# Output gate tiles computed inside the attentions of a two-half even mixer, with negated maxima held in SBUF

## The reference, cut to what matters

```
aq, ak, av, ag, bq, bk, bv, bg = split_cols(h @ w_in, EVEN_WIDTHS)   # 8 query, 2 key/value heads each
# A: rms_norm of q and k, rope; every query block attends to the context and all latent tokens
# B: rope; a block attends to the context and to its own and its two neighbour blocks, with a sink
s = einsum(q, k) * ATTN_SCALE (+ bias);  p = softmax(s);  o = einsum(p, v)
y = concatenate([oa * silu(ag), ob * silu(bg)]) @ w_out
```

## Time and profile before

| | us |
|---|---|
| median of 3 runs | 3201.89 (3201.58 to 3202.61) |
| the profiled execution, its own time | 3198.09 |
| its span | 3196.3 |
| TensorE busy | 3028.5 (95%) |
| VectorE busy | 1480.0 (46%) |
| ScalarE busy | 761.3 (24%) |
| GpSimd busy | 596.5 (19%) |

### The profile page before, as it was taken

The page is one execution under the profiler, slowest core; times in us unless marked ns, Lnnn a source line. Parts: engine busy times, 40 slices in busy tenths (PEclk is TensorE's granted clock), DMA queues, the critical chain, the costliest instruction groups (busy, mean ns, idle before and its releaser), DMA issues.

```text
span 3196.3 us, 27666 instructions
## 1 busy us (share of the span) xinstructions
PE 3028.5 (95%) x11326; PEld 1554.0 (49%) x11326; DVE 1480.0 (46%) x1858; ACT 761.3 (24%) x923; POOL 596.5 (19%) x394
## 2 busy tenths in 40 slices
PE   7998898997889999999999999999999999999997
PEld 4563445653455545444774545454444444444443
DVE  4636873248846586735773311035453343340001
ACT  4116662005410210113641122122012222220000
POOL 0004673003410122233441000000112222210000
PEclk9999998999889899999999899999999999999998
DMA  6001000020033211123221001100211111112101
GB/s 222 27 27 40 1 1 7 27 87 1 1 121 110 112 40 40 40 68 80 55 91 45 30 20 40 33 27 20 92 40 43 50 40 41 52 50 89 36 36 53
DMA packets 41071, 162.42 MB, mean 51 GB/s; under 512 B 5265, under 2 KB 5777, under 8 KB 36721
## 3 DMA queue, kind: packets, MB, share of 16 engines
q1 hardware_dynamic: 34704, 143.18, 12.8%
q0 software_dynamic: 6240, 17.47, 2.2%
HBM read 148.04 MB, written 15.20 MB: 51 GB/s over the span
## 4 chain that ended last, share of the span: by engine, by line
PE 86%; DVE 7%; ACT 3%; issue 2%; POOL 1%; DMA 1%; SPq 0%; DVEq 0%; ACTq 0%; POOLq 0%
PE ps L794 28%; PE ps L787 20%; PE ps L1433 9%; PE ps L1319 4%; PE ps L1272 3%; PE ps L1206 2%; PE ps L1056 2%; PE ps L969 2%; PE ps L1089 2%; PE ps L984 2%; PE ps L998 2%; PE ps L1108 1%; PE ps L902 1%; DVE x_ctx L2046 1%; DVE arena L2046 1%
## 5 line engine op out<-in xcount | busy, mean ns | idle before, releaser
L787 PE MATMUL ps<-arena 128*128 128x512 f32 (+1 forms) x1632 | 625.6, 544 | 15.8 <-ACT arena L1485 10.9
L787 PEld LDWEIGHTS ps<-arena 128*128 128x128 f32 x1632 | 311.5, 192 | 321.0 <-issue 306.8
L794 PE MATMUL ps<-arena 128*128 128x512 f32 x936 | 411.3, 592 | 3.2 <-DVE arena L2248 1.6
L794 PE MATMUL ps<-x_lat,arena 128*128 128x512 f32 x688 | 303.9, 592 | 0.0
L794 PEld LDWEIGHTS ps<-arena 128*128 128x128 f32 x936 | 177.6, 190 | 227.2 <-issue 223.8
L1433 PE MATMUL ps<-arena 128*128 128x512 f32 x616 | 264.5, 592 | 0.0
L794 PEld LDWEIGHTS ps<-x_lat,arena 128*128 128x128 f32 x688 | 130.7, 190 | 164.5 <-issue 164.5
L1056 PE MATMUL ps<-arena 64*128 64x512 f32 x504 | 152.7, 687 | 49.6 <-DVE x_ctx L2046 23.8
L1433 PEld LDWEIGHTS ps<-arena 128*128 128x128 f32 x616 | 117.0, 190 | 147.3 <-issue 147.3
L2223 DVE SCALAR_TENSOR_TENSOR x_ctx<-arena,vectors,x_ctx 128x1024 f32<-128x1024 f32 x120 | 169.6, 1413 | 3.5
L1468 ACT ACTIVATE arena<-x_lat 128x1024 f32<-128x1024 f32 x40 | 42.0, 1050 | 465.7 <-DVEq L2177 343.3
(11 more groups left out here) (284 smaller groups left out, 4137.3 us busy)
## 6 DMA issues: line engine op xcount, KB each, us to landing
arena<-in_wall SPq DMA_DIRECT2D x188, 512.0 KB, 3.8
arena<-in_wdown SPq DMA_DIRECT2D x7, 1408.0 KB, 6.0
x_lat<-in_xl_in SPq DMA_DIRECT2D x8, 1024.0 KB, 9.5
residual_store<-x_lat SPq DMA_DIRECT2D x8, 1024.0 KB, 6.8
x_lat<-residual_store SPq DMA_DIRECT2D x8, 1024.0 KB, 8.6
x_lat<-expanded_bias POOLq DMA_DIRECT2D x48, 160.0 KB, 3.6
arena<-expanded_bias POOLq DMA_DIRECT2D x32, 160.0 KB, 4.0
out<-x_lat SPq DMA_DIRECT2D x8, 512.0 KB, 3.0
```

Of the source, the lines that this page charges most:

```text
L787: mm = pe.matmul(ps[:, o + c:o + c + n], W[:, ring_of(g) % WSLOTS, k, :], rhs(k, c, n), start=(k == 0), stop=(k == KT - 1))
L794: mm = pe.matmul(ps[:, bank * BANK:(bank + 1) * BANK], weights[:, k, :], tokens[:, k, :], start=(start and k == 0), stop=(k == 3), skip_gr ...
```

## The change

Gate tiles 1 to 3 of each half leave the product stage. They are cut into nine pieces: for each of the token ranges 0 to 511, 512 to 1023 and 1024 to 1279, one piece for each of the three tiles. Piece 0 is computed ahead of the attention's first fill. Pieces 1 and 2 are spread over the steps before the first broadcast. Pieces 3 to 8 follow the broadcasts of groups 0 to 5, one each, between the broadcasts. They use the banks of `NM_BC`; to free these, ScalarE copies the negated maxima to SBUF (`NMS`), and the subtraction reads them there. Pieces 0 to 2 get their Silu as they are evacuated; 3 to 5 and 6 to 8 are copied out, and one Silu over three rows follows each set. The late rows are computed beside q, k, v and gate 0 of half B, with the weight order of evB changed to match, and ScalarE copies out the v tiles of both halves. Some semaphores of other stages are merged.

```diff
+EVB_ORDER = ["q0", "L0", "L1", "q1", "L2", "q2", "L3", "q3", "L4", "k", "L5", "v", "g0", "L6", "L7", "g1", "g2", "g3"]
+EVB_WALL = ["q0", "q1", "q2", "q3", "k", "v", "g0", "L0", "L1", "g1", "L2", "L3", "g2", "L4", "L5", "g3", "L6", "L7"]
+GATE_PIECES = [(m, c, n) for c, n in ((0, 512), (512, 512), (LAT, CTX)) for m in (1, 2, 3)]
+
+
+def gate_evacuated(p):
+
+    return p + 1 + (p >= 6)
+
+
+def gate_plan(steps):
+
+    nb = [i for i, st in enumerate(steps) if "NB" in st]
+    for i in range(nb[0] - 1):
+        a, b = 16 * i // (nb[0] - 1), 16 * (i + 1) // (nb[0] - 1)
+        steps[i]["GU"] = [(1 + u // KT, u % KT) for u in range(a, b)]
+        for u in range(a, b):
+            if u % KT == KT - 1:
+                steps[i + 1]["GE"] = 1 + u // KT
+    steps[0]["GE"] = 0
+    for p in range(3, len(GATE_PIECES)):
+        at, width = nb[p - 3], nb[p - 2] - nb[p - 3] - 2
+        for k in range(KT):
+            steps[at + 1 + k * width // KT].setdefault("GU", []).append((p, k))
+        steps[at + 1 + width]["GE"] = p
+        if p % 3 == 2:
+            steps[at + 2 + width]["GS"] = p // 3
...
-        MASK_PREV, MASK_NEXT = area(SCR + 6656, P), area(SCR + 6656 + P, P)
+        NMS = area(SCR + 6 * 1024, 1024)
+        MASK_PREV, MASK_NEXT = area(SCR + 7 * 1024, P), area(SCR + 7 * 1024 + P, P)
...
+                for m, name in enumerate(("q0", "q1", "q2", "q3", "k")):
+                    product((ph, "qk", m), even_weight(ph, name), hrow, full,
+                            (lambda k: (h_ready, k + 1)) if first and m == 0 else None)
                     if first and m >= 1:
                         ssq(m - 1)
-                wait_weight(g0 + 5)
+                    if not first and m in (2, 4):
+                        late_modulation(m - 2, 2)
+                gv = even_weight(ph, "v")
...
-                for m in range(4):
-                    g = g0 + 6 + (m if first else 3 * m)
-                    product((ph, "gate", m), g, hrow, full)
-                    if not first:
-                        late_modulation(2 * m, 2)
+                else:
+                    late_modulation(4, 2)
+                product((ph, "gate", 0), even_weight(ph, "g0"), hrow, full)
+                if not first:
+                    late_modulation(6, 2)
...
+                def gate_part(p, k):
+                    m, c, n = GATE_PIECES[p]
+                    o = NM_BC + (p % 2 if p < 3 else 0) * BANK
+                    if k == 0:
+                        wait_weight(even_weight(ph, f"g{m}"))
+                        if p == 2:
+                            pe.wait_ge(at["gate_out"], 1)
+                        if p >= 3:
+                            pe.wait_ge(at["spread"], p - 2)
+                            pe.wait_ge(at["gate_out"], gate_evacuated(p - 1))
+                    mm = pe.matmul(ps[:, o:o + n], W[:, even_weight(ph, f"g{m}") % WSLOTS, k, :], H[:, k, c:c + n],
+                                   start=(k == 0), stop=(k == KT - 1))
+                    if k == KT - 1:
+                        mm.then_inc(at["gate_in"], 1)
+
+                for k in range(KT):
+                    gate_part(0, k)
+                pe.wait_ge(qk_done, 5 if ph == "evA" else 10)
+                pe.wait_ge(v_ready, 10 if ph == "evA" else 20)
                 fill(0)
                 for st, ahead in zip(at["plan"], at["plan"][1:] + [{}]):
...
-                        pe.wait_ge(at["neg_max"], g + 1)
+                        pe.wait_ge(*((at["sink_in"], g + 1) if at["sink"] else (at["reduced"], 2 * g + 2)))
+                        pe.wait_ge(at["gate_out"], gate_evacuated(min(g + 2, len(GATE_PIECES) - 1)))
                         if g:
-                            pe.wait_ge(at["shifted"], first[g])
+                            pe.wait_ge(at["spread"], g)
                         for h in range(HEADS):
                             mm = pe.transpose(ps[:, NM_BC + h * P:NM_BC + (h + 1) * P],
                                               ST[:, g % 4, 1, h:h + 1].to_broadcast([P, P]), IDENT)
                         mm.then_inc(at["bcast"], 1)
+                    for p, k in st.get("GU", ()):
+                        gate_part(p, k)
...
+                for i in range(TOK // P):
+                    t, o = ready(ph, "v", i)
+                    if i == 0 and not first:
+                        act.wait_ge(soft["A"]["pv"], len(soft["A"]["items"]))
+                    act.activation(VE[:, i, :], ps[:, o:o + P], ACT.Copy).then_inc(ps_free[t % 2], 1)
+                    act.wait_ge(ps_free[t % 2], t // 2 + 1)
+                    act.nop().then_inc(v_ready, 1)
...
-                for m in range(4):
-                    t, o = ready(ph, "gate", m)
-                    act.activation(G[:, (0 if first else 4) + m, :], ps[:, o:o + TOK], ACT.Silu).then_inc(ps_free[t % 2], 1)
+                t, o = ready(ph, "gate", 0)
+                act.activation(G[:, 0 if first else 4, :], ps[:, o:o + TOK], ACT.Silu).then_inc(ps_free[t % 2], 1)
...
+                    if "GE" in st:
+                        p = st["GE"]
+                        m, c, n = GATE_PIECES[p]
+                        o = NM_BC + (p % 2 if p < 3 else 0) * BANK
+                        act.wait_ge(at["gate_in"], p + 1)
+                        act.activation(G[:, rows + m, c:c + n], ps[:, o:o + n], ACT.Silu if p < 3 else ACT.Copy)\
+                           .then_inc(at["gate_out"], 1)
+                    if "GS" in st:
+                        c, n = GATE_PIECES[3 * st["GS"]][1:]
+                        act.wait_ge(at["gate_out"], gate_evacuated(3 * st["GS"] + 2))
+                        act.activation(G[:, rows + 1:rows + 4, c:c + n], G[:, rows + 1:rows + 4, c:c + n], ACT.Silu)\
+                           .then_inc(at["gate_out"], 1)
...
+                    if "NB" in st:
+                        g = st["NB"]
+                        act.wait_ge(at["bcast"], g + 1)
+                        if g:
+                            act.wait_ge(at["shifted"], at["first"][g])
+                        act.activation(NMS, ps[:, NM_BC:NM_BC + 1024], ACT.Copy).then_inc(at["spread"], 1)
...
-                for i in range(0 if first else TOK // P):
-                    t, o = ready(ph, "v", i)
-                    if i == 0:
-                        dve.wait_ge(soft["A"]["pv"], len(soft["A"]["items"]))
-                    dve.tensor_copy(VE[:, i, :], ps[:, o:o + P]).then_inc(ps_free[t % 2], 1)
-                    dve.wait_ge(ps_free[t % 2], t // 2 + 1)
-                    dve.engine_nop().then_inc(v_ready, 1)
-                for m in range(0 if first else 4):
-
-                    late_rows(2 * m, 1)
-                    late_rows(2 * m + 1, 1)
-                    dve.wait_ge(w_mod, MOD0 + 2 * m + 2)
-                    dve.tensor_tensor(MOD[:, 0, MOD0 + 2 * m:MOD0 + 2 * m + 2, :],
-                                      ps[:, TB:TB + 8].rearrange("p (m a d) -> p m a d", a=2, d=2)[:, :, :, 0],
-                                      vcol("mod_b", MOD0 + 2 * m, 2).unsqueeze(2).to_broadcast([P, 2, 2]), ALU.add)\
-                       .then_inc(late_mod_read, 1)
+                        if m in (2, 4):
+                            late_gate_rows(m - 2)
+                        for i in ((0, 1), (2,), (3,), (4,), (5,))[m]:
+                            late_rows(i, 1)
+                if not first:
+                    late_gate_rows(4)
+                    late_rows(6, 1)
+                    late_rows(7, 1)
+                    late_gate_rows(6)
...
-                        dve.wait_ge(at["bcast"], g + 1)
+                        dve.wait_ge(at["spread"], g + 1)
                     p = ring[n % len(ring)]
-                    dve.tensor_tensor(p, ps[:, NM_BC:NM_BC + 1024], p, ALU.add).then_inc(at["shifted"], 1)
+                    dve.tensor_tensor(p, NMS, p, ALU.add).then_inc(at["shifted"], 1)
...
+                        dve.wait_ge(at["gate_out"], 3 if g < 4 else 7 if g < QT else 11)
...
-                        dve.wait_ge(at["reduced"], 2 * g + 2)
                         if at["sink"]:
+                            dve.wait_ge(at["reduced"], 2 * g + 2)
                             link(dve.tensor_tensor(nm, nm, NSINK[:, :], ALU.min))
                             dve.tensor_tensor(ST[:, g % 4, 3, :], nm, vcol("sink", 0, 8), ALU.add).then_inc(at["sink_in"], 1)
-                        dve.engine_nop().then_inc(at["neg_max"], 1)
```

More of the change, by code:

```diff
@@ L64, in wall_tile @@
 def wall_tile(g):
-    i = g - GBASE["od"]
+    i, j = g - GBASE["od"], g - GBASE["evB"]
+    if 0 <= j < len(EVB_ORDER):
+        return GBASE["evB"] + EVB_WALL.index(EVB_ORDER[j])
     return GBASE["od"] + OD_WALL[i] if 0 <= i < len(OD_WALL) else g
@@ L80, in product_tiles @@
             out.append((ph, "ssq", 4))
-        out += [(ph, "gate", m) for m in range(4)]
+        out.append((ph, "gate", 0))
     out += [("evO", "res", m) for m in range(KT)]
@@ L128, in group_plan @@
         steps.pop()
+    gate_plan(steps)
```

(43 more changed lines are left out.)

33 lines of the change are left out of this document (11 added, 22 removed).

## The result

The changed kernel takes 3213.79 us (median of 6 runs, 3209.14 to 3218.94), the kernel before 3201.73 beside it (6 runs, 3198.36 to 3202.61). The ratio is 1.0039, 95% interval 1.0027 to 1.0052: slower by 0.4%. I had forecast 3188 and gave "slower" 0.31. The time lies inside the range, the direction is wrong.

The account below looks back on a forecast made before the run. TensorE, 95% busy, was taken to bound the kernel. A at +9.5 us and B at -23.3 made -13.8: profiled 3198.1 becomes 3184.3, or 3188 on the median of runs, range 3145 to 3230.

Parts of the forecast that it names:

- 2 x 4.0: Attention A, groups 6 and 7, without gate pieces: each 4.0 us longer, 34.0 against the steady 30.0.
- 9 x 3.33 + 2.26 = 32.2: An A group: least time for nine subtraction and GpSimd add pairs that exclude each other, 32.2 us.
- the lock: VectorE's two-SBUF-input subtraction and GpSimd's SBUF-reading add exclude each other: 3.33 us a pair, up to 1.07 per add.
- 2 x 34.1 + 3 x 30.6: A's groups 1 to 5: TensorE time per group, 34.1 us with a 512-column piece, 30.6 with a 256-column one.
- the Silus' 4.0: Two three-row Silus on ScalarE per attention, 0 to 4.1 us each, taken as 2: +4.0 us an attention.
- 2 x 2.4 + 3 x 4.1 = 17.1: A's groups 1 to 5: subtraction and add contention beyond TensorE's time, 36.5 against 34.1 and 34.7 against 30.6.
- the prologue and group 0: First fill to first denominator: +7.0 and +6.5 us in A, +5.9 and +4.7 in B, idle TensorE absorbing the rest.
- Rival 1: Every add meets a subtraction: A's groups +76.8 us instead of 41.6, total 3238, slower; chance 0.20.
- Rival 2: Subtractions slip in between adds without harm, TensorE sets A's groups: -48 us, 3154; chance 0.20.
- Rival 3: Gate steps hide nothing, pieces 1 to 8 count in full: +28 us in A, +23 in B, 3239; chance 0.12.
- 0.5 a group: Attention B: subtractions rarely meet GpSimd's four adds, so contention costs 0.5 us a group, from 0 to 4.3.
- The v stall of 3.1: evB's v stage: 3.1 us wait for VectorE rotating k disappears, as ScalarE copies v out.

Follow-up runs that it names:

- before_sbuf_max: Kernel before plus only ScalarE's copy of the negated maxima to SBUF, read there by the subtraction; gates stay in the product stage: 3254.7 us, ratio 1.0176.
- after_psum_tail: Changed kernel, but from group 6 on, in A and B, the subtraction reads the negated maxima from PSUM without the copy: 3183.47 us, ratio 0.9951.
- after_write: Changed kernel with GpSimd's additions of probabilities replaced by constant writes of about the same time that read nothing: 3155.52 us, ratio 0.986.
- after_thin_pieces: Changed kernel with six of the eight contraction steps of pieces 3 to 8 left out: 3191.12 us, ratio 0.9976.
- before_write: Control: kernel before with GpSimd's additions of probabilities replaced by writes that read nothing: 3185.15 us, ratio 0.9949.

## Why the prediction was wrong

- **The step that failed is "2 x 4.0" for A's last two full groups**, in "groups: 3 x 6.5 + 3 x 4.7 + 2 x 4.0 = 41.6". I set every group against the 30.0 us of the steady ones. Groups 6 and 7 took 27.1 and 18.8 before, since in the drain the fills and maxima run out: group 6's stretch has half of them, group 7's none. In the changed kernel they take 33.3 and 32.2. The floor that I had worked out, 9 x 3.33 + 2.26 = 32.2, was right to about 2 us (before_sbuf_max has 30.4 and 34.5), and it shows most where there is the least to hide it; the difference was taken from the wrong base. Measured +19.5 instead of +8.0. after_psum_tail takes the copy out of the drains alone, gives back 21.2 us in A and 6.8 in evB and B, and turns the sign.
- **Groups 1 to 5 of A:** right. Without the lock (after_write) they take 164.24 us; TensorE's 2 x 34.1 + 3 x 30.6 and the Silus' 4.0 make 164.0. The lock adds 17.9 (182.17 - 164.24), where I had 2 x 2.4 + 3 x 4.1 = 17.1.
- **A second step failed, of 6.5 us in A and 7.3 in B: the prologue and group 0.** I let TensorE's idle 7 to 8 us of the prologue take up pieces 1 and 2, and group 0's slack most of piece 3, so that of 20.6 us of matmuls (3 x 6.9) 13.5 would count in A and 10.6 in B. It was 20.0 and 17.9. The prologue, first fill to first subtraction, took 34.2 in A where I had 32.5, with TensorE busy all but 0.1 us of it, and 29.2 in B where I had 26.0, with 2.5 us of TensorE still idle (my base of 20.1 there held the 0.7 us wait that I had already taken off elsewhere). From the first subtraction to the first denominator it took 50.4 in A (39.2 before) and 37.0 in B (29.1). In A that is the lock: before_sbuf_max, with the copy and no piece at all, has 50.8, and after_thin_pieces, with a quarter of piece 3, has 50.2. I had put only 2.4 us of lock into this group. (Piece 3 would show without the lock: 44.2 in after_write, 37.9 in before_write.) In B it is piece 3: after_thin_pieces has 28.3 there, less than before the change, so group 0 of B had no slack for it. Up to the first fills the sums held within 0.8 and 2.6 us, which is inside the scatter.
- **The lock and its rival sizes:** the mechanism was right, and the price in A was 41 us, where the forecast had 30.5 (17.1, 2.4 in group 0, 8 and 3). Rival 1's mean group of 36.9 was not reached (groups 1 to 7 have 35.4 on the mean), and the pure lock kernel has 33.2 to 35.2 in groups 1 to 5. Rival 2's 3154 is near after_write's 3155.52, but by chance: its fair partner is 3185.15, and the change's gain without the lock is 29.6, not 48. Rival 3 holds in B more than in A.
- **The rest of evB and B:** +13.8 instead of +14.6. The lock costs B nothing on balance (0.5 a group taken), as it was paid there before in the minimum with the sink; in the last latent group, which has no fills, it does cost 3.6. The v stall of 3.1 went as forecast.
- **Later stages:** +6.0 with the same instructions. Most of it is scatter between profiles and not the change's: the stages after B take 2278.7 us in before, but 2281.5 in before_sbuf_max and 2283.7 in before_write, which both have evB's old order and all gates in the product stage. TensorE's busy time there moves as well (2218.1 in before, 2224.6 in the changed kernel, 2222.3 in before_write, 7330 recorded matmul instructions each). But the six kernels with nine pieces in B lie at 2283.9 to 2285.2 and the six others at 2278.7 to 2283.7, so 1 or 2 us may belong to the change. A and B account for 7.8 of the 12.1 us between the medians, and what the rest is stays open.

The Trainium skill (SBUF — State Buffer, "Who interferes with whom") says that a VectorE instruction with two SBUF inputs contends with a GpSimd instruction that reads SBUF, and not with one that only writes it. The traces agree: with GpSimd's reads exchanged for writes the subtraction never lasts over 1226 ns (after_write), with them up to 3.37 us, and once 5.21. I weighed the rule and took it into the sum; what I missed were the places where it has no cover.

## What to carry to other kernels

A floor that a new lock or wait sets has to be compared with each stage's own length, the short drain above all, and not with the steady state's. A copy that frees a PSUM bank also changes which memory the next instruction reads: here it put a two-SBUF-input VectorE instruction beside GpSimd's additions, which costs 1.05 us a time (3.31 instead of 2.26). Keep the PSUM operand where that engine pair is dense, and use the copy only where it is sparse (B). Small instructions count too: a 128x8 minimum with two SBUF inputs lasted up to 2.17 us in the kernel before, and freed from GpSimd's reads B was 13 us shorter.

## What the runs showed of the hardware

- A DMA issue on GpSimd (3.43 us) did not slow a VectorE instruction with two SBUF inputs when memsets came behind it (1.22 us, after_write). With an addition behind it the subtraction at 239.97 lasted 5.21, past the issue from 238.20 and the addition's 2.46 from 241.63, and in before_sbuf_max it was the same 5.21. With the issue moved away it lasted 3.29, beside the addition alone. So an addition waiting behind the issue seems to hold VectorE off before it runs; no run separates this further.
- When such a pair alternates, an independent VectorE instruction that reads PSUM is free: subtraction 2.25 plus maximum 1.21 at a pitch of 3.31, and 3.1 to 3.3 without the maximum.
- In the drain of the changed kernel TensorE's granted clock was 0.85 and 0.75 of full speed (mixtures of 1.2 and 2.4 GHz), with its matmuls spread over 33.3 and 32.2 us. In after_psum_tail nearly the same matmuls came in 25.5 and 18.8 us, and the clock was 1.00; TensorE's busy time in the second group was 14.47 instead of 19.76. Even at the lower clock TensorE was idle for 12.4 of the 32.2 us, so the pair of VectorE and GpSimd and not the clock is the likelier cause of the length; no run holds the clock fixed.
